# Decode attention of a hybrid trunk: where the probabilities are turned, and in which buffers the value pages land

## The reference

```
q, k, v, g, iq, ik, iw = dsa_project(rmsnorm(ys, dsa_norm[j]), dsa_w_in[j])
o = dsa_sample_attend(q, k, v, iq, iw, ik, cache_k[j], cache_v[j], cache_idx_k[j], page_table)
ds = dsa_out(o, g, dsa_w_out[j])        # (o * silu(g)) @ w_out
...
s = einsum('bqhd,bqkhd->bqhk', q, k_sel) * HEAD_DIM ** -0.5      # top 256 of 1028 keys by the indexer
p = softmax(where(valid, s, -inf))
o = einsum('bqhk,bqkhd->bqhd', p, v_sel)
```

## Time and profile before

| | |
|---|---|
| median of 3 runs | 1153.78 us (1153.21 to 1155.95) |
| profiled execution, its time | 1151.64 us |
| profiled execution, its span | 1149.9 us |
| TensorE busy | 1112.4 us, 97% |
| VectorE, ScalarE, GpSimd busy | 59%, 43%, 33% |
| granted TensorE clock | 0.998 of full speed |
| read from and written to memory | 150.70 and 16.81 MB, 146 GB/s over the span |

### The profile page before, as it was taken

How to read it: one execution, slowest core, us unless ns; L and a number is a source line. 1 busy time by engine, 2 the same in 40 slices (tenths; PEclk the granted TensorE clock), 3 DMA queues, 4 the chain that set the end, 5 groups by cost and what they waited for, 6 DMA issues and landing times. The chain is left out here.

```text
span 1149.9 us, 25599 instructions
## 1 busy us (share of the span) xinstructions
PE 1112.4 (97%) x10579; PEld 974.7 (85%) x10579; DVE 675.2 (59%) x1215; ACT 494.7 (43%) x968; POOL 383.1 (33%) x321
## 2 busy tenths in 40 slices
PE   7999999899999999999999999999999999999897
PEld 6889888899758988879945499999999889888796
DVE  6462255854999779777444555595544362255742
ACT  6542376643443322222354553322553451466643
POOL 5545213243313423114300134453354245312230
PEclk9999999999999999999999999999999999999999
DMA  5335233333314787884789923224220335233302
GB/s 169 103 111 165 92 111 113 127 84 99 118 50 153 241 277 235 275 311 138 255 326 407 383 74 106 64 89 130 80 75 3 111 110 165 75 129 111 100 30 78
DMA packets 127787, 168.81 MB, mean 147 GB/s; under 512 B 20384, under 2 KB 93480, under 8 KB 127663
## 3 DMA queue, kind: packets, MB, share of 16 engines
q1 hardware_dynamic: 115609, 152.59, 39.9%
q10 hardware_dynamic: 12062, 14.59, 3.6%
HBM read 150.70 MB, written 16.81 MB: 146 GB/s over the span
## 5 line engine op out<-in xcount | busy, mean ns | idle before, releaser
L737 POOL TENSOR_TENSOR w_lo<-raw,w_hi 128x512 fp32r<-128x512 f32 (+2 forms) x267 | 360.7, 1381 | 688.8 <-ACT w_hi L1501 688.7
L773 PE MATMUL psum<-h_hi,w_hi 128*128 128x272 f32 x1616 | 471.2, 292 | 6.6 <-DVE h_lo L2425 4.7
L775 PE MATMUL psum<-h_hi,w_lo 128*128 128x272 f32 x1616 | 467.3, 289 | 0.0
L774 PE MATMUL psum<-h_lo,w_hi 128*128 128x272 f32 x1616 | 464.8, 288 | 0.0
L773 PEld LDWEIGHTS psum<-h_hi,w_hi 128*128 128x128 f32 x1616 | 303.3, 188 | 20.2 <-issue 15.3
L774 PEld LDWEIGHTS psum<-h_lo,w_hi 128*128 128x128 f32 x1616 | 303.7, 188 | 0.1
L775 PEld LDWEIGHTS psum<-h_hi,w_lo 128*128 128x128 f32 x1616 | 303.0, 187 | 0.0
L1501 ACT ACTIVATE w_hi<-raw 128x1024 fp32r<-128x1024 f32 (+1 forms) x137 | 135.5, 1034 | 116.8 <-PE psum L775 79.5
L773 PE MATMUL psum<-w_hi,h_hi 128*128 128x512 f32 (+2 forms) x352 | 124.1, 353 | 1.2 <-DVE dsa_score_s L2519 0.8
L775 PE MATMUL psum<-w_hi,h_lo 128*128 128x512 f32 (+2 forms) x352 | 121.0, 344 | 1.8 <-issue 1.8
L774 PE MATMUL psum<-w_lo,h_hi 128*128 128x512 f32 (+2 forms) x352 | 121.0, 344 | 0.7 <-issue 0.7
(11 more groups left out here) (331 smaller groups left out, 1366.2 us busy)
## 6 DMA issues: line engine op xcount, KB each, us to landing
smp_keys<-in_cache_k_dram SPq DMA_DIRECT2D x128, 256.0 KB, 4.9
raw<-in_gla_w_in_dram SPq DMA_DIRECT2D x23, 1024.0 KB, 5.4
spare<-in_cache_v_dram SPq DMA_DIRECT2D x36, 512.0 KB, 7.2
raw<-in_dsa_w_in_dram SPq DMA_DIRECT2D x17, 1024.0 KB, 5.3
raw<-in_cache_v_dram SPq DMA_DIRECT2D x28, 512.0 KB, 8.7
gla_s_in<-in_state_gla_dram SPq DMA_DIRECT2D x16, 512.0 KB, 7.9
raw<-in_gla_w_out_dram SPq DMA_DIRECT2D x8, 1024.0 KB, 6.7
out_dram<-gla_s_in ACTq DMA_DIRECT2D x16, 512.0 KB, 4.6
```

The costliest lines, as they stand in the source:

```text
L737: pool.tensor_tensor(copies(key, pair_view(w_lo, key)[:, k]), raw_copies(key, k), copies(key, pair_view(w_hi, key)[:, k].bitcast(F32)), AL ...
L773: pe.matmul(out, lh, rh, start=start, stop=False)
L774: pe.matmul(out, lh, rl, start=False, stop=False)
L775: return pe.matmul(out, ll, rh, start=False, stop=stop)
```

## The change

- `turn_probs` and `probs_out` are cut in three parts. Group 0 is turned at jobs 36, 37, 38 (banks 6, 7, 6) instead of at job 43, group 1 at n = 5, 6, 7 in bank 5 instead of at n = 15 in banks 0, 1, 2.
- `smp_pt` is no tile of its own any more: ScalarE writes the turned probabilities back over the part of `smp_p` that they came from, so that each group has its own.
- Pages 0 and 1 are multiplied ahead of jobs 41 and 43, pages 2 to 15 at n = 1, 3, ..., 27.
- `rows_out` moves from n = 15 and 31 to 12 and 28, `turn_out` with `sample_branch` from 17 and 33 to 14 and 30.
- `free_from` counts the spare buffers that job group g 3 holds as given up later. V5, V6, V7 take raw buffers (of V0, V1, V2), V8 that of V3, V9 and V10 the two spare ones of g 3; before, V5 and V6 waited for those.
- out 0 comes behind V31 in the list instead of behind V29. Its split on ScalarE moves from n = 26 to n = 30.

```diff
+TURN_AT, EARLY_AT = (36, 37, 38), (41, 43)
+TURN_LATE = (5, 6, 7)
+PAGE_AT = tuple(range(1, 28, 2))
+ROWS_AT, OUT_TURNED = (12, 28), (14, 30)
...
-        pt_s = d("smp_pt", [P, NPAGE, P])
+        d.o += size([P, NPAGE, P], F32)
...
-        ptn_s = d("smp_ptn", [NS, P])
+        ptn_s = [d("smp_ptn", [NS, P]), at("smp_ptn1", [NS, P], F32, pt_s_at)]
+        pt_s = [t[:, 0:PAST].rearrange("p (g r) -> p g r", r=P) for t in p_s]
...
                     items.append(((L, "V", i), None, 2, D, "V"))
-                    if i == 4 * NPAGE - 3:
+                    if i == 4 * NPAGE - 1:
                         f_item((L, "out", 0), dsa_w_out[j], 0, HALF)
...
             if s >= RAW and items[index[held_by[s]]][4] == "w":
-                return index[first] - 1 + 0.1 * held_by[s][2], s
+                return index[first] + (2 * len(EARLY_AT) - 0.5 if held_by[s][2] == 3 else -0.5), s
...
                     if f == len(FILL) - 1:
                         page_bias(1)
-                        turn_probs(0, (6, 7, next_bank(range(2))))
+                    if f in TURN_AT:
+                        turn_probs(0, TURN_AT.index(f), (6, 7, 6)[TURN_AT.index(f)])
+                    if f in EARLY_AT:
+                        value_page(0, EARLY_AT.index(f))
                     project(f)
...
                 for n in range(N + 3):
-                    if n == 2 * NPAGE - 1:
-                        turn_probs(1, (0, 1, 2))
-                    if n in (2 * NPAGE + 1, 4 * NPAGE + 1):
-                        turn_out(n // (4 * NPAGE))
+                    if n in TURN_LATE:
+                        turn_probs(1, TURN_LATE.index(n), 5)
+                    if n in OUT_TURNED:
+                        turn_out(OUT_TURNED.index(n))
                     if n < N:
                         scores(n)
-                    if (n == 0 or n % 2) and n < 4 * NPAGE - 1:
-                        value_page((n + 1) // (2 * NPAGE), (n + 1) // 2 % NPAGE)
+                    if n in PAGE_AT:
+                        value_page(*divmod(PAGE_AT.index(n) + len(EARLY_AT), NPAGE))
...
-                    if n == 2 + last_spare[0][2] // 2 * 2:
+                    if n == len(units) - 2:
                         split_hi(pair_of[(L, "out", 0)])
```

More of the change, by code:

```diff
@@ L1338, in page_bias, with turn_probs @@
                     mm.then_inc(*sig("page_scores", L, grp))
-                def turn_probs(grp, banks):
+                def turn_probs(grp, x, bank):
                     by_seq = ident[:].rearrange("p (c b x) -> p b c x", c=4, b=4)
                     pe.wait_ge(*on("p_norm", L, "sample", grp))
[L1344 to L1352, removed]
+                    b = claim(bank, ("PsT", L, grp, x), ("pt_s", L, grp, x))
+                    if x < 2:
+                        for pg in range(4):
+                            o = (4 * x + pg) * PAGE
+                            mm = pe.matmul(psum[:, b, pg * P:(pg + 1) * P], p_s[grp][:, o:o + PAGE], by_seq, start=True, stop=True)
+                    else:
+                        mm = pe.matmul(psum[0:NS, b, 0:P], p_s[grp][:, PAST:KEYS], by_seq, start=True, stop=True)
+                    mm.then_inc(*sig("PsT", L, grp, x))
@@ new lines, in value_page @@
+                def value_page(grp, pg):
+                    keys = [(L, "V", (grp * NPAGE + pg) * 2 + y) for y in range(2)]
+                    if pg == 0:
+                        pe.wait_ge(*on("pt_s", L, grp, 2))
+                        for half in range(2):
+                            claim(6 + half, ("Os", L, grp, half), (f"o_full{half}", L, grp))
+                    for key in keys:
+                        pe.wait_ge(*on(f"raw{slot[key]}", key))
+                    for half in range(2):
+                        for bl in range(4):
+                            r = slice(bl * NS, (bl + 1) * NS)
+                            o = (bl % 2) * D + half * BLK
+                            mm = pe.matmul(psum[r, 6 + half, :], pt_s[grp][:, pg, r], held(slot[keys[bl // 2]])[:, o:o + BLK],
+                                           start=pg == 0, stop=False)
+                    mm.then_inc(*sig("pages_used", keys[0], also=((keys[1],),)))
+                    if pg == NPAGE - 1:
+                        for half in range(2):
+                            for bl in range(4):
+                                r = slice(bl * NS, (bl + 1) * NS)
+                                mm = pe.matmul(psum[r, 6 + half, :], ptn_s[grp][:, r],
+                                               v_d[0:NS, SMP, half * BLK:(half + 1) * BLK], start=False, stop=True)
+                        mm.then_inc(*sig("Os", L, grp))
@@ L1395, in values_of @@
                     mm.then_inc(*sig("O", L, n))
[L1397 to L1419, removed]
                 def turn_out(grp):
@@ L1917, in sample_exp, with probs_out @@
                                    accum_out=ast[:, 3 + grp, 2:3]).then_inc(*sig("p_exp", L, "sample", grp))
[L1919 to L1927, removed]
+                def probs_out(grp, x):
+                    act.wait_ge(*on("PsT", L, grp, x))
+                    b = bank_of("PsT", L, grp, x)
+                    if x < 2:
+                        copy(pt_s[grp][:, 4 * x:4 * x + 4, :], psum[:, b, :].rearrange("p (g r) -> p g r", g=4))\
+                            .then_inc(*sig("pt_s", L, grp, x))
+                    else:
+                        copy(ptn_s[grp][:], psum[0:NS, b, 0:P]).then_inc(*sig("pt_s", L, grp, x))
                 last_early = max(p for p in range(2 * NPAGE) if PAIR_AREA[p] == 0)
@@ L1938, in dsa @@
                         scores_out(1)
-                        probs_out(0)
+                    if f in TURN_AT:
+                        probs_out(0, TURN_AT.index(f))
                     if f == 26:
@@ L1971, in dsa @@
                         sample_exp(1)
[L1972 to L1976, removed]
+                    if n in ROWS_AT:
+                        rows_out(ROWS_AT.index(n))
+                    if n in TURN_LATE:
+                        probs_out(1, TURN_LATE.index(n))
+                    if n == OUT_TURNED[1] + 1:
                         act.wait_ge(*on("os_read", L, 1, 1))
@@ L2632, in dsa @@
                         sample_norm(1)
[L2633 to L2636, removed]
+                    if n in ROWS_AT:
+                        rows_out(ROWS_AT.index(n))
+                    if n in OUT_TURNED:
+                        sample_branch(OUT_TURNED.index(n))
                     if n < len(units):
```

## The result

The changed kernel takes 1157.44 us (median of 12 runs, 1155.83 to 1160.80), the kernel before beside it 1153.52 us (12 runs): a ratio of 1.0027, 95% interval 1.0017 to 1.0037; the medians lie 3.9 us apart. The forecast was 1153.3 us, no change that can be told. In a second comparison the same two kernels gave 1159.16 and 1154.73 us, 1.0035 (1.0023 to 1.0048). So the change costs some 0.3%, and the mechanism has to be found for about 4 us.

The account below looks back on a forecast made before the run. It took TensorE as nearly full and the DMA engines as wholly full; gains of 5.7 us less costs of 5.2 gave net -0.5 us, median 1153.3 us, no change that can be told, range 1149.5 to 1157.5.

Parts of the forecast that it names:

- the forecast's own range: Total time if the forecast's main case, no change that can be told, holds: 1151 to 1156 us, chance 0.55.
- the end chain: Scores of unit 30 to the first product of the output projection: 9.7 us before, expected to reach 660.23 + 11.8.
- h_lo: End, VectorE's subtraction: slowed where it meets GpSimd's w_lo pieces, between 0 and 1.1 us, taken as 0.6.
- the normalise: Unit 31 on VectorE: might also wait for a GpSimd piece, some 0.5 us worse; left out of the sum.
- The late exp: Unit 31 on ScalarE: two splits and a copy stand ahead of the last exp, making it 1.5 us late.
- its rival: Waits at the end and start of the units drop the clock to 1.2 GHz: 6 us, 1159.3 us, chance 0.08.
- `turn_out` at 0.9 us: Group 1, moved ahead of the scores of unit 30: no longer fills a wait and costs its full 0.94 us.
- The page waits: TensorE's waits for value pages among the units: all 3.6 us counted as gone.
- the last page: Page 15 waiting for V31: about 2 us of slack expected; rival that it comes late, 1159.3 us, chance 0.04.
- The DMA hole: DMA rate near nothing from about 571.6 to 579.4 us, 7.8 us; two items of 2.65 us expected to fill it.
- switches: Restarts of TensorE where turned blocks break jobs at five places instead of one: 0.5 us (bounds 0 and 1.0).
- The first turn: Before unit 0 is turned, TensorE waits for normalised probabilities with one page as cover instead of two: 1.7 us.

Follow-up runs that it names:

- e11: The changed kernel itself, measured and profiled once more with no edit: 1159.16 us, ratio to the kernel before 1.0035.
- e5: The kernel before with only the split of out 0 moved from unit 26 to unit 30: 1159.4 us, ratio to the kernel before 1.0039.
- e8: The changed kernel with GpSimd's w_lo pieces of out 0 held until VectorE has normalised unit 31: 1154.96 us, ratio to the kernel before 1.0010.
- e3: The changed kernel with three unneeded products put in each of TensorE's two last waits: 1155.58 us, ratio to the kernel before 1.0015.
- e1: The changed kernel with the removed next_bank call taken back, so the last job falls on bank 1: 1156.18 us, ratio to the kernel before 1.0027.
- e9: The kernel of e8 once more, for a second profile: 1156.20 us, ratio to the kernel before 1.0011.
- e4: The changed kernel with the split of out 0 at unit 28 and turn_out of group 1 back at n = 33: 1152.16 us, ratio to the kernel before 0.9985.
- e6: The changed kernel with out 0 back ahead of V30 in the list and its split at unit 26: 1160.7 us, ratio to the kernel before 1.0049.
- e2: The changed kernel with the split of out 0 at unit 28 instead of 30: 1152.94 us, ratio to the kernel before 0.9990.

## Why the prediction was wrong

The 1157.44 us lie above the forecast's own range of 1151 to 1156, and at the edge of the whole one (1149.5 to 1157.5).

**The step that failed: the end chain**, "the exp starts near 665.8: 1.5 us late", with 0.6 for h_lo and nothing for the normalise and the clock. I had 9.7 + 2.1 = 11.8 us and it took 14.5. The mechanism was named and half of it was priced:

- The late exp was right. From ScalarE's free moment (664.99) the splits take 1.99 - 0.10 and the copy 0.3 us, and the exp starts 2.2 us later; before it started 0.76 us after the same point. That is 1.4 us against 1.5.
- h_lo was right: 1.27 - 0.69 = 0.6 us, the value taken.
- The normalise was left out because one row did not decide it. It took 1.29 instead of 0.49 us: 0.8 us more, in both profiles of the changed kernel (1.30 in e11) and in e5, and nothing in e8. The bound of 0.5 us was too small. The Trainium skill, SBUF — State Buffer, "Who interferes with whom", lets tensor_scalar in a two-port mode be blocked too, and the trace agrees.
- The clock was priced at nothing and its rival given 0.08. It cost 1.9 us (e3). The waits that it named were right (1.8 and 1 to 2 us forecast, 1.62 and 1.75 measured). The argument against it, that one wait of 2.2 us had left the clock at 1.00 before, was one case of something that goes both ways: waits of 1.6 to 1.7 us brought the fall in the changed kernel, in e5 and at the first turn of e1, and left the clock at 1.00 in e8, e9 and e11. So a single profile without a fall is no reason for a price of nothing. The Trainium skill, TensorE: Matmul & The Clock Gate, Part 1, has the clock at half after idle time, and the trace agrees in that it stood at 0.50 behind the wait. The rival's size of 6 us was too large, because only one place fell, not two, and the half clock did not last through the projection.

With 1.9 + 0.8 = 2.7 us more, the end term would have been right (4.8 against 4.8), and the forecast 1156.0. `turn_out` at 0.9 us is a term of its own, ahead of unit 30. Its block does take that time there, but with the split at 28 moving it back gains nothing (e4); with the split at 30 no run moved it alone.

**The page waits**, "I count all 3.6 us of page waits as gone": 2.2 went and 1.4 stayed (pages 14 and 15). I gave the last page 2 us of slack by counting only the transfer of V31 and out 0 behind page 13. But V31 was issued from 642.4 us on, and page 15 could start on it at 650.8, 8.4 us later, for 2.6 us of its own transfer: the DMA engines were full, and I read the rest as the items still ahead of it. No run separates these from out 0, issued 1.2 us behind it. TensorE came to page 15 after 8.0 us from page 13 (I had 7.5), so the time to it was right and the time of the transfer was not. e6 met the same with 5 us.

**What went as forecast.** The DMA hole is nearly closed: what was 7.8 us is about 1.5 us under 150 GB/s. The rate in 40 slices of 571 to 586 us, as the earlier trace rows:

```profile
GB/s 404 197 273 262 382 350 382 339 350 415 284 339 360 328 404 382 393 470 382 459 404 382 470 360 240 142 55 55 33 186 208 284 393 339 273 306 339 284 142 175
```

The start up to unit 0 took 4.6 us more, against 3.7 for two pages + 0.5 of switches. The wait of 0.58 us for the flipped bank, which I had not seen, is in it, so some 0.3 us is left for the switches. The first turn waited 1.19 us; with the 0.58 at unit 0, which delays TensorE ahead of it, that is 1.8 us against 1.7. The claim of a bank at page 8 (0.55 us, for the copies of `rows_out`) is a second wait that I had not listed; the view names no releaser for it, and VectorE's copy of these rows ends just ahead of it (618.4 us), so that it belongs to the change is an inference; no run took it away.

**The balance.** From the key scores of job 35 to the projection the forecast had -0.5 us, and the profile shows +4.35 (e11: +3.5). By stretches: the end has 4.8 instead of 2.1 (the clock and the normalise); the units have -5.1 instead of the -6.8 that the forecast's terms leave for them (mostly 1.4 for the pages and 0.55 for page 8, less the 0.5 by which the first turn waited shorter); the start has 4.6 instead of 4.2. The change without its split, e2, stands at -0.8 us: nearly the -0.5 of the forecast, for reasons that partly cancel, since its end is 2.1 us cheaper and its pages dearer than I had them.

**The chances.** Slower had 0.13. The split at the end should have been a rival of its own: "the chain's operations meet GpSimd's pieces, TensorE waits for them, and behind a wait the clock falls".

## What to carry to other kernels

A ScalarE or GpSimd operation put "where the engine is idle" costs what it delays in a latency chain: move it to a place where TensorE still has its own work (unit 28 instead of 30 was worth the whole loss). Where a change leaves TensorE a new wait of 1.5 us or more, price the fall of the clock (1.9 us here) by a chance, even if a longer wait left the clock alone in one profile, and try a few useless products in the wait. When a later transfer must meet an earlier deadline, count the bytes still queued ahead of it at the moment it is issued, not only its own.

## What the runs showed of the hardware

**The same wait brings a fall of the clock in one execution and not in the next.** In a table of 46 stretches of 25 us, eleven of the thirteen profiles have one to three with 0.93 where others have 1.00, nearly always at the same places (50 to 75, 500 to 525, 900 to 925 us), which no edit touched; the fall in e1 from 587.5 us on is one more of them. (The last stretch, 1125 to 1150 us, has 0.89 to 0.98 in eight profiles and is not counted.) Kernel e9, whose profiled execution was the slowest of its 12 (1157.80 us), has all three, e8, the same kernel, none:

```profile
500.00:525.00 25.00, 22.99 (x393) 20.37 (x393) 17.85 (x23) 4.68 (x10) 3.11 (x3) 0.93 0.81 280
900.00:925.00 25.00, 24.47 (x166) 20.28 (x165) 7.08 (x12) 11.46 (x22) 8.70 (x6) 0.93 0.37 123
50.00:75.00 25.00, 25.00 (x131) 19.94 (x131) 20.92 (x32) 11.90 (x15) 12.35 (x9) 0.93 0.14 43
```

Each is a stretch of about 3.5 us at half clock (0.07 x 25 / 0.5), and costs up to 1.7 us. None of these three comes in the middle of steady work. The table in steps of 1 us shows TensorE idle at 509 us, ahead of the fall in 500 to 525 (1.86 us in all), and the fall a good microsecond after the work has begun again:

```profile
509.00:510.00 1.00, 0.00 (x0) 0.00 (x0) 0.93 (x4) 0.00 (x0) 0.00 (x0) 1.00 0.98 389
511.00:512.00 1.00, 1.00 (x10) 1.00 (x9) 0.93 (x3) 0.00 (x0) 0.00 (x0) 0.89 1.05 415
512.00:513.00 1.00, 1.00 (x7) 1.00 (x7) 1.00 (x1) 0.00 (x0) 0.00 (x0) 0.50 1.04 373
```

Ahead of the other two stand waits of only 0.53 us (at 48.0 and 918.0 us), each followed by a block of eight products with 16 rows. The kernel before and the changed kernel have the wait at 509 us too, 1.8 and 1.9 us, without a fall. Falls go with the scatter between executions of one kernel: of the 29 of the kernel before beside e9, those with a mean clock of 0.993 took 1157.0 to 1158.2 us, those with 0.998 took 1151.0 to 1153.2. This is why one profile can't price a fall.

**VectorE beside GpSimd.** A normalise (tensor_scalar) of 0.49 us took 1.29 to 1.30 us in the kernels whose pieces of `w_lo` ran then (changed, e1, e3, e5, e11), as the two-input subtraction did (1.15 to 1.28 instead of 0.69), and 0.49 us in e8, where they were held. In e2, whose pieces run from 660.0 us on, a normalise beside them took 0.89 us, off the critical chain. I had not expected it of an operation with one tensor input.
